# Output projection, norm and router in one stage, six experts held, page sums in both projections

## What is computed

```python
xp = xp + yp                                  # yp = mixer(rms_norm(x)) @ w_out
xp = xp + hier_moe(rms_norm(xp, ln_ffn[layer]), *mw)
...
grp_prob = softmax(x2 @ w_grp + b_grp); grp_w, grp_i = top_k(grp_prob, 1)
exp_logits = (x2 @ w_exp + b_exp).reshape(-1, N_GROUPS, EXPERTS_PER_GROUP)
top_l, top_i = top_k(in_grp, TOP_K_IN_GROUP)  # two experts of the best group
h = silu(x2 @ w_gate) * (x2 @ w_up); y = (h * combine) @ w_down
```

## Time and profile before

| what | value |
|---|---|
| median of 3 runs | 2151.22 us (2150.83 to 2152.65) |
| profiled execution | 2150.78 us, span 2149.0 us |
| PE busy | 1638.4 us (76%) |
| DVE, ACT, POOL busy | 790.3, 494.2, 181.0 us |
| mean granted TensorE clock | 0.857 |
| DMA | 443.41 MB, mean 206 GB/s |

### The profile page before, as it was taken

One profiled execution on the slowest core, in us unless ns is written; L12 is line 12 of the kernel. 1 busy time (PEld: TensorE's weight loads), 2 busy tenths in 40 slices (PEclk: granted clock), 3 DMA queues, 4 the chain that ended last, 5 costly groups with the idle time before them and its releaser, 6 DMA issues. The chain is left out here.

```text
span 2149.0 us, 35773 instructions
## 1 busy us (share of the span) xinstructions
PE 1638.4 (76%) x12824; PEld 1195.2 (56%) x12824; DVE 790.3 (37%) x1836; ACT 494.2 (23%) x1250; POOL 181.0 (8%) x282
## 2 busy tenths in 40 slices
PE   4999977888697487775898477875766687487875
PEld 3888866677486244444777355652433376354443
DVE  1666323556302211112155537665544302211112
ACT  2111751222102011111000046773111101111110
POOL 0000003112100311110000000000000000211110
PEclk8999977998597699987799768997787788699997
DMA  3555425200117399992499610006899526299995
GB/s 112 184 173 181 158 79 197 83 5 4 62 59 285 112 426 425 423 407 103 142 313 314 227 63 1 2 2 222 321 343 331 195 69 272 66 424 424 424 422 200
DMA packets 130596, 443.41 MB, mean 206 GB/s; under 512 B 22001, under 2 KB 27634, under 8 KB 112562
## 3 DMA queue, kind: packets, MB, share of 16 engines
q1 hardware_dynamic: 114274, 421.77, 51.7%
q0 software_dynamic: 11008, 17.89, 2.3%
q10 hardware_dynamic: 5200, 2.23, 0.4%
HBM read 426.35 MB, written 43.77 MB: 219 GB/s over the span
## 5 line engine op out<-in xcount | busy, mean ns | idle before, releaser
L1903 PE MATMUL moe_experts_bank_gu<-moe_weights_gu,moe_experts_xT 128*64 128x256 f32 x2048 | 258.4, 416 | 66.5 <-DMA moe_weights_gu<-in_w_gate_up 50.1
L1903 PEld LDWEIGHTS moe_experts_bank_gu<-moe_weights_gu,moe_experts_xT 128*64 128x64 f32 x2048 | 170.6, 151 | 165.8 <-issue 117.5
L408 PE MATMUL proj_acc<-h_gdn,proj_w 128*128 128x272 f32 x1024 | 238.0, 395 | 13.9 <-DMA proj_w<-in_gdn_w 13.9
L408 PEld LDWEIGHTS proj_acc<-h_gdn,proj_w 128*128 128x128 f32 x1024 | 195.8, 191 | 54.9 <-DMA proj_w<-in_gdn_w 14.3
L2143 PE MATMUL nproj_acc<-nsa_h,nproj_w 128*128 128x272 f32 x640 | 151.0, 396 | 11.2 <-DMA nproj_w<-in_nsa_w 11.2
L2143 PEld LDWEIGHTS nproj_acc<-nsa_h,nproj_w 128*128 128x128 f32 x640 | 120.8, 191 | 41.1 <-DMA nproj_w<-in_nsa_w 17.0
L1924 PE MATMUL moe_experts_bank_y<-moe_weights_down,moe_experts_hT 128*64 128x512 f32 x512 | 116.9, 598 | 25.8 <-ACT moe_experts_hT L1953 25.8
L1984 DVE SCALAR_TENSOR_TENSOR moe_experts_h<-moe_experts_bank_gu,moe_table,moe_experts_gate 128x128 f32<-128x128 f32 x64 | 22.5, 351 | 300.0 <-ACT moe_experts_gate L1948 300.0
L282 DVE TENSOR_REDUCE nsa_past_c<-nproj_raw 128x4096 f32 x20 | 88.4, 4420 | 113.2 <-DMA nproj_raw<-in_cmp_pool 113.2
L1656 POOL DMA_INDIRECT table<-moe_router_entry,moe_router_slot_of x20 | 19.2, 962 | 997.1 <-DVE moe_router_place L1614 991.6
L282 DVE TENSOR_REDUCE first_sums<-proj_raw 128x1536 f32 (+1 forms) x32 | 56.1, 1753 | 92.1 <-DMA proj_raw<-in_cmp_pool 92.1
(11 more groups left out here) (487 smaller groups left out, 2582.8 us busy)
## 6 DMA issues: line engine op xcount, KB each, us to landing
moe_weights_gu<-in_w_gate_up SPq DMA_DIRECT2D x64, 2048.0 KB, 20.9
moe_weights_down<-in_w_down SPq DMA_DIRECT2D x64, 1024.0 KB, 22.5
ring_kv<-in_slc_pool SPq DMA_DIRECT2D x256, 256.0 KB, 5.0
nproj_raw<-in_cmp_pool SPq DMA_DIRECT2D x160, 256.0 KB, 4.3
proj_raw<-in_cmp_pool SPq DMA_DIRECT2D x96, 256.0 KB, 2.8
proj_w<-in_gdn_w SPq DMA_DIRECT2D x32, 512.0 KB, 3.2
nproj_w<-in_nsa_w SPq DMA_DIRECT2D x20, 512.0 KB, 5.9
moe_results_y<-y_rows SPq DMA_DIRECT2D x16, 512.0 KB, 6.8
```

The source lines that it names most:

```text
L408: mm = pe.matmul(acc[s][:, a, 0:HALF], w[s][:, k, :], g.hT[:, k, a * HALF:(a + 1) * HALF], start=(k == 0), stop=(k == KT - 1))
L1903: mm = pe.matmul(gu_bank[m][H, 0:FF], ln.xT[:, k, H], w.gu[:, k, m * FF:(m + 1) * FF], start=(k == 0), stop=(k == KT - 1))
```

## The change

The output projection, the norm behind it and the router become one stage, `moe_front_stage`. In it ACT squares each residual tile as it comes, DVE adds the squares up, PE sums them once; the logits are computed logit-major (16 calls of 272 columns), block by block behind the gains, and turned by five small transposes. The counts take four calls, after four additions over tiles on DVE. The number of passes is worked out behind the table entries. Norm and router reuse buffers of the projection. SP loads a piece of expert weights behind each load of output weights from the third on, and the rest after the last.

Weights of six experts are held (three slots of a pair); a slot is reloaded when its pair is done. The pairs are written out instead of looped over, SP's reloads too. `ExpertWeights` takes fixed addresses. The activations of a lane share one room, one of them in `g.mix`, which replaces `zT` and `attT`.

Page sums: 5 for a convolution tile, 7 for a z tile (176 pages in GDN), 4 for an NSA tile (80). In GDN a lane's pages are asked for behind the other lane's weights.

Constants come in three sets; those of a mixer load in the norm ahead of it.

```diff
+MOE_SLOTS = 3
+CONST_SETS = {
+    "consts": ("ident", "ones", "head_ones", "first_pick", "before", "first_slot", "token", "swap"),
...
-PAGES_GDN = 3
-PAGES_NSA = 8
-PAGES_EARLY = PAGES_GDN * (CONV_TILES + HEADS)
+PAGES_CONV, PAGES_Z, PAGES_NSA = 5, 7, 4
+PAGES_CONV_END = PAGES_CONV * CONV_TILES
+PAGES_EARLY = PAGES_CONV_END + PAGES_Z * HEADS
...
+                def load_weights(s, i):
+                    sp.wait_ge(pe_s[s].sem, pe_s[s].past("product", i))
+                    sp.dma_start(w[s][:, :, :],
+                                 g.d["gdn_w"][bass.ds(2 * i + 2 + s, 1)].rearrange("t p k c -> (t p) k c")
+                                 ).then_inc(loaded[s], 16)
...
+                conv_pages(0, 0)
+                with sp.Fori(0, rounds - 1) as i:
+                    load_weights(0, i)
+                    conv_pages(1, i)
+                    load_weights(1, i)
+                    conv_pages(0, i + 1)
+                load_weights(0, rounds - 1)
+                conv_pages(1, rounds - 1)
+                load_weights(1, rounds - 1)
+                z_pages(0, 0)
+                for i in range(z_rounds):
+                    if i < z_rounds - 1:
+                        load_weights(0, rounds + i)
+                    z_pages(1, i)
+                    if i < z_rounds - 1:
+                        load_weights(1, rounds + i)
+                        z_pages(0, i + 1)
                 for s in range(2):
                     sp.wait_ge(pool_s[s].sem, pool_s[s].past("sample tail", rounds - 1))
                 sp.dma_start(g.d["conv_out"], tails[:, :, :]).then_inc(stored, 16)
...
-def out_project_stage(nc, g, name, w_d, src):
...
+def moe_front_stage(nc, g, name, w_d, w, bias, load_router, load_piece):
...
+                def gather_squares(m):
+                    dve.wait_ge(squared, m + 1)
+                    if m >= 2:
+                        dve.wait_ge(gathered, m - 1)
+                    dve.tensor_tensor(squares[:, :], squares[:, :], sq[m % 2][:, :], ALU.add).then_inc(gathered, 1)
+                for m in range(KT):
+                    dve.wait_ge(multiplied, m + 1)
+                    dve.tensor_tensor(halves(g.xT[:, m, :]), acc[m % 2][:, :, 0:HALF], halves(g.xT[:, m, :]),
+                                      ALU.add).then_inc(added, 1)
+                    if m >= 2:
+                        gather_squares(m - 1)
+                gather_squares(KT - 1)
+
+                dve.wait_ge(inverted, 1)
+                for k in range(KT):
+                    dve.scalar_tensor_tensor(out=hT[:, k, :], in0=g.xT[:, k, :],
+                                             scalar=g.gains[:, g.ffn_gain + k:g.ffn_gain + k + 1], in1=rms[:, :],
+                                             op0=ALU.mult, op1=ALU.mult).then_inc(normed, 1)
+
+                dve.wait_ge(router_in, 32)
...
+                in_group = grp[:, :, :].unsqueeze(3).broadcast_to([P, NT, GROUPS, PER_GROUP])
+                step(dve.tensor_tensor(by_group(at_pick[:, :, :]), by_group(logits[:, :, GROUPS:]), in_group, ALU.mult))
+                step(dve.tensor_reduce(inside[:, :, :], at_pick[:, :, :].rearrange("p t (k e) -> p t e k", e=PER_GROUP),
+                                       AX_X, ALU.add))
...
+                for m in range(2):
+                    sp.dma_start(wo[m][:, :, :], w_d[m]).then_inc(loaded[m], 16)
+                load_router(sp, router_in)
                 sp.wait_ge(cleared, 1)
                 sp.dma_start(g.d["table"], empty[:, :, :]).then_inc(emptied, 16)
+                for m in range(2, KT):
+                    sp.wait_ge(multiplied, m - 1)
+                    sp.dma_start(wo[m % 2][:, :, :], w_d[m]).then_inc(loaded[m % 2], 16)
+                    load_piece(sp, m - 2)
+                for n in range(KT - 2, 4 * MOE_SLOTS):
+                    load_piece(sp, n)
...
             @block.scalar
...
+                for m in range(KT):
+                    act.wait_ge(added, m + 1)
+                    if m >= 3:
+                        act.wait_ge(gathered, m - 2)
+                    out = squares if m == 0 else sq[m % 2]
+                    act.activation(out[:, :], g.xT[:, m, :], ACT.Square).then_inc(squared, 1)
...
+                pe.wait_ge(gathered, KT - 1)
+                for a in range(2):
+                    mm = pe.matmul(total[:, a, 0:HALF], g.const("ones"), squares[:, a * HALF:(a + 1) * HALF],
+                                   start=True, stop=True)
+                mm.then_inc(summed, 1)
+                pe.wait_ge(router_in, 32)
+                for k in range(KT):
+                    pe.wait_ge(normed, k + 1)
+                    for a in range(2):
+                        mm = pe.matmul(logit_acc[0:n_log, a, 0:HALF], w[:, k, :], hT[:, k, a * HALF:(a + 1) * HALF],
+                                       start=(k == 0), stop=(k == KT - 1))
+                mm.then_inc(logits_done, 1)
...
+                for t in range(3):
                     turn(t)
...
+                every = slice(0, NT * EXPERTS)
+                pe.matmul(counts[:, every], g.const("before"), picked[:, :, :].rearrange("p t n -> p (t n)"),
+                          start=True, stop=False)
+                pe.matmul(counts[:, every], g.const("ones"), tiles_ahead[:, :, :].rearrange("p t n -> p (t n)"),
+                          start=False, stop=True)
+                pe.matmul(cn[:, NT, :], g.const("ones"), tiles_ahead[:, TILES, :], start=True, stop=False)
+                pe.matmul(cn[:, NT, :], g.const("ones", NEW), picked[0:NEW, TILES, :], start=False, stop=True
+                          ).then_inc(counted, 1)
+                for t in range(3, NT):
+                    turn(t)
...
+        def weights_of(pair):
+            slot = pair % MOE_SLOTS
+            return weights[2 * slot:2 * slot + 2]
...
+                def load(pair, freed):
+                    ln = lanes[freed[1] % MOE_LANES]
+                    last_round = freed[0] * rounds + freed[1] // MOE_LANES
                     sp.wait_ge(ln.pe.sem, ln.pe.past("gate up 1", last_round))
-                    for w in ln.w:
-                        w.load_gate_up(sp, i)
+                    for w in weights_of(pair):
+                        w.load_gate_up(sp, pair // MOE_SLOTS)
                     sp.wait_ge(ln.pe.sem, ln.pe.past("down", last_round))
...
+                for pair in range(MOE_SLOTS, PAIRS):
+                    load(pair, (0, pair - MOE_SLOTS))
```

476 lines of the change are left out of this document (229 added, 247 removed).

## The result

The changed kernel takes 2047.16 us (median of 4 runs, 2041.07 to 2051.38); the kernel before takes 2151.93 us beside it (4 runs, 2150.83 to 2154.78). The ratio is 0.9509 (0.9483 to 0.9535), a gain of 105 us where 120.6 was forecast: faster as forecast and inside the range of 2014 to 2060, but 17 us over the forecast of 2030 and 3 us over the bracket of 2016 to 2044, to which 0.70 was given. The profiled execution is the slowest of the four, 2051.38 us with a span of 2049.2.

What follows compares the result with a forecast made beforehand. Stages run one after another, each with its own limit: transfer at the start, SyncE in the NSA projection, small waits before the experts, bytes in them. 3.4 + 27.4 + 46.1 + 43.7 = 120.6 off 2150.8 gives 2030 us, range 2014 to 2060.

Steps and rivals of the forecast that it cites:

- Start: Input load before the first norm: 1.456 MB less of constants at 426 GB/s, 3.4 us gained.
- NSA projection: Products 7.33 us apart instead of 8.11 with four pages a lane, and a shorter SyncE tail: 27.4 us gained, between 25 and 30.
- GDN projection: Takes the 80 pages, hidden by PE's 7.33 us per tile: costed at nothing, bounds 0 to +5 us.
- Front stage: Last residual add to the router's first scatter: 29 us instead of 53.0, 24 us gained a layer, 17 to 25.
- I take 2.4 GHz and add 1 us: Logits in the router: 7.33 us at the 2.4 GHz level plus 1 us, with ends 0 and +7.3.
- rival A: PE stays at 1.2 GHz in logits and last pair: +6.3 and +6 us a layer at most, 2055; chance 0.13.
- A's other half: PE at 1.2 GHz in the last pair of experts: +6 us a layer at most.
- rival B: Pieces of expert weights hold up the output weights: 19.8 us a layer, 2070; chance 0.09.
- Experts, the pair: Six experts held when the expert stage starts, so one pair less to load behind it: 14.9 us gained a layer.
- the longer program: Loops over expert pairs written out, so instructions must be fetched: bounds 0 to 10 us in all, taken as 0.
- Experts, the tail: Last bytes to results stage: last gate and up product starts as its weights land, 7.2 and 4.8 us gained.
- Rival C: Page requests ahead of weight loads close the GDN projection's ring (16.4 us becoming over 22): slower, 2162 at 44 us; chance 0.03.

Runs made afterwards that it cites:

- the two-slot kernel: Weights of four experts held instead of six, all else as in the changed kernel: 2076.90 us, 28.0 us slower than the changed kernel run once more.
- the kernel without rows: Changed kernel without row gathers after the first two pairs and without scatters, results stage reading the normed rows twice instead: 1997.83 us.

## Why the prediction came out as it did

- **Start**: right in its place (3.5 us at the first square), but 1.5 us went back at once. Of TensorE's 32 calls in the sum the first 13 took 6.1 us and the other 19 only 4.5; before, the slow start was 3.2 us long. The calls became short at 19.85 us and before at 20.50, nearly the same moment, though the sum began 3.5 us sooner. The forecast carried the saved transfer through as if the norm behind it kept its length. That the slow start is the lower clock isn't shown: the trace's first record of the granted clock, 1.00, begins at 19.84 us (20.37 before).
- **NSA projection**: right, 27.2 for 27.4, each step of it: 7.33 us a product, the last request a microsecond ahead of the end, the tail moved by 12 to 14. Undone, 25.7 come back.
- **GDN projection**: right, 1.2 us for 0 (0 to 5); the sum of five pages took 2.81 us against the bound of 2.92.
- **Front stage**: 22.8 and 22.1 for 24. The step that failed is "I take 2.4 GHz and add 1 us": the granted clock fell in pauses of 2.3 and 2.4 us too, and the logits took 10.4 us, not 8.3 (10.3 in layer 1), so rival A came true here by some 2 of its 6.3 us. The rest of the chain was 1 us shorter than costed. A's other half, the last pair, didn't occur: its product took 7.13 us at a granted clock of 1.00. The pieces cost nothing, as costed, and rival B didn't occur.
- **Experts, the pair**: right, 14.5 and 13.6 us for 14.9 by undoing it. The estimate by the Trainium skill's "DMA: Bandwidth & Descriptors", Specifications (17.6 us at 358 GB/s) falls with that. The rest of the pair's gain went to the stage's start: from the read of the table to the next stage's first instruction are 4.9 to 5.4 us where there were 4.1, in the traces with the pairs written out, the two-slot kernel's too (6.0 and 6.2 where the table is read in two parts). It lies inside the 0 to 10 us allowed for the longer program; that it is the fetch of instructions isn't shown.
- **Experts, the tail**: wrong, and this is the 12 us. The step that failed is "pair 15 started at 968.64, 2.8 us behind the last bytes". The 965.8 was the time at which the bytes would have been through had DMA kept its full rate; the window 960 to 970 at 247 GB/s and the one behind it were an engine-by-engine end, with the last gate and up weights landing at 968.2 and the last down weights at 973.2. Results came 15.8 us behind that last landing before and 15.2 us after (14.9 and 15.2 in layer 1), so next to nothing was left to gain. The sign named for it, DMA full until some 15 us ahead of the results, didn't come: it is full until 924, 29 us ahead of the read at 952.87. Three slots couldn't give what was there already, and undoing them brings no tail back.
  "Perfetto Trace Analysis" of the Trainium skill, DMA Instruction — HWDGE (DVE, Sync), says that every DMA engine begins and ends its own part and that the semaphore has its value only when all have reported; the landings above agree, up to 15 us apart.
- **Rival C** didn't occur: the ring of the GDN projection stayed open.
- **The range** held the time, but in part by luck: 2030 was the likeliest case because the tail seemed certain, and the upper part, made for rival A, took in 12 us of a tail that wasn't there.

## What to carry to other kernels

The end of a stream isn't where its bytes divided by its rate end: read the landing of the last transfer that the consumer waits for, and compare it with the consumer's start, in the kernel before, ahead of promising a shorter tail. A chain of short steps that is made shorter runs at whatever clock its waits leave, so cost its TensorE calls at both levels, and remember that a few products that nobody reads can be cheaper than the lower level. A stream that many DMA engines share ends with the busiest of them, so count the bytes of small transfers beside it engine by engine, not in sum.

## What was not expected of the hardware

- The parts of one 2 MiB transfer landed within 2.0 us of each other when weights alone moved for 28 us (in the kernel without rows the last of them within 3.2), and up to 14.9 us (16.5 in layer 1) when rows of 4 KB moved beside them for 13 pairs, while DMA as a whole ran at 420 to 430 GB/s. With only four experts' weights held (the kernel before, and the run with four) it was 10.5 and 10.9 us.
- Where a row of an indirect transfer lies has a part in which engine carries it: a layout of the same rows over other partitions put half of the DMA engines some 27 us behind the other half, at 207 to 220 GB/s, and for the two layouts printed in full above the 16 delays of layer 0 follow from a count of rows within 2.3 us.
- One program's executions differed by up to 20 us (2044.71 to 2064.19) with the same instructions; in the two traces that were compared most of the difference goes with the granted clock. The kernel before differed by up to 12 us within a set of 7 runs (2145.72 to 2157.44).
